# Groups of few units alternate with full ones, z gets a third buffer, and side tiles whose inputs are missing let others pass

## The chip, the cores and the metric

The kernel runs on all 8 cores of one Trainium2 chip. Each core computes half of the tokens of one of the four sequences (2048 rows out of 4096: every second block of 128), and no core talks to another. The metric is the device time of the slowest core in microseconds (us). A core has TensorE (PE in the profile), VectorE (DVE), ScalarE (ACT), GpSimd (POOL) and SyncE (SP). They run side by side and wait for each other by semaphores.

## What is computed

```python
h = rms_norm(x, g_pre)
proj = h @ w_in                                  # w_in: 1024 x 6144
q, k, v, z_a, cb, cc, cx, z_c, ga, gc = jnp.split(proj, idx, axis=-1)
# branch A: differential attention, 4 heads, two softmax maps each, ALiBi, causal
s = einsum(q, k) * scale - slope[h] * (qpos - kpos)
a = softmax(s[map 0]) - lam * softmax(s[map 1])
o = rms_norm(a @ v, subln_gain) * (1 - lam_init)
y_attn = (o * silu(z_a)) @ w_attn_o
# branch B: width-3 causal depthwise convolution, gated
u = causal_depthwise_conv(cc * cx, conv_w)
y_conv = ((cb * u) * silu(z_c)) @ w_conv_o
# merge and output
y = sigmoid(ga + b_a) * y_attn + sigmoid(gc + b_c) * y_conv
out = x + rms_norm(y @ w_out, g_post)
```

## The kernel before

The program is recorded first and played later. `Prog.op` appends an operation to the list of its engine, works out its semaphore waits from the names that it reads and writes, and keeps a rough clock of its own for each engine (`p.now`), from an assumed duration `t` for every operation. The planner's decisions (what stands next on PE, when a piece of DVE work is put in) are taken from that clock while the program is built. On the chip the order of each engine is fixed.

**Stages.** (1) Up to about 156 us: norms of x, transposes, and the projections to V, K and Q. (2) From 156 to 547 us: attention, the subject here. (3) Merge gates and branch outputs (L1428, L1435), up to 713 us. (4) Output projection (L1481) and the final norm.

**The attention stage.** Its work is cut into 16 groups, one for a stripe s of 512 query rows and a head h. A group is a run of units. One unit is a score matmul over key blocks (L1099), an exponential on ACT (L1128), on the causal edge a mask on DVE (L1140), and the product with V (L1159). Stripe 0 has 3 units; stripe 3 has 15 for heads 2 and 3. Heads 0 and 1 have steep ALiBi slopes, so their far blocks are left out and their groups are short: 3 units for (0, 0), 5 for (3, 0). `GROUPS` is the order of the groups. Scores fill PSUM banks 0 to 3, and the sums over V sit in banks 4 to 6.

**Side tiles.** ACT has more to do for a unit than PE, so PE takes other matmuls between units: tiles from one list, `fill.q`, all of which use the only bank left, bank 7. They are `kq` (L725, remaining Q and K projections), `norm` (L907, only before the fork), `conv` (L823, 8 matmuls of 512 columns, 64 tiles), `halo` (L954, 16 matmuls of 32 columns), `z` (L858, 32 matmuls of 128 columns, the silu gate's input for one group) and `trans` (L1239, 4 transposes of a group's gated output; its result is copied out at L1246). `put_fill` takes from the head of the list until PE's planned time reaches the next unit, and `credit` spreads the tiles over the stage.

**The end of a group.** `epilogue` (L1186 to L1204) sums and scales the accumulators on DVE, and must be through before the next group's L1159 may write banks 4 to 6. It then puts the rest on the list `side`: four squares (L1213), `rstd` (two small operations on DVE, L1219 and L1221, and a power on POOL, L1223), four gates (L1231), which read `oraw`, the POOL result and `sz`, and `trans`. `z` has its own tail: a tanh on ACT (L870), a multiplication (L872), later the gain (L878). Pieces of `side` and `chain` are put on DVE where the planner sees room.

**Two buffers.** `oraw`, `gat` and `sz` have two buffers, taken in turn by the number g of the group. So a group's `trans` must be done before the epilogue of the group two later, and `epilogue` begins with this:

```python
while g >= 2 and g - 2 not in t_done:
    fill.step()
```

It takes side tiles one after the other, with whatever waits they have, until `trans` of g - 2 is through. And z's tile of group g is held back in `z_wait` until nothing of group g - 2 is left on `side`, since both use the same half of `sz`:

```python
if z_wait and not any(x[0] <= g - 2 for x in side):
    fill.push(z_tile(*z_wait))
```

Up to the first four groups (heads 2 and 3, stripes 3 and 0) the norms of Q and K are measured beside the attention; behind them a register decides between two versions of the rest (the fork; its value is read behind L943). The version that runs here leaves out the far blocks.

Of the kernel before, what the change touches and what calls it, by code (L numbers as in the profile page):

```python
# [289 lines left out]
def build_program():  # L290
# [23 lines left out]
    with contextlib.ExitStack() as st:  # L314
        K = 1024
# [3 lines left out]
        def emission(p, skip):  # L319
# [14 lines left out]
            def take(n):  # L334
                nonlocal o
                r = o
                o += (n + 63) // 64 * 64
                return r
# [70 lines left out]
            sz_off = take(4 * K)  # L409
            sz = [reg(sz_off + i * 2 * K, 2 * K, F32).rearrange("p (b n) -> p b n", b=4) for i in range(2)]  # L410
            gc_off = take(16 * K)
# [10 lines left out]
            zr_off = [take(2 * K) for _ in range(2)]  # L422
            tz_off = take(2 * K)
            tz = reg(tz_off, 2 * K, F32)
            zr = [reg(a, 2 * K, F32) for a in zr_off]
# [52 lines left out]
            for i in range(2):  # L478
                for d in range(4):
                    p.place(("hTp", i, d), htp_off[i], 8 * K)  # L480
                p.apart([("hTp", i, d) for d in range(4)])
                p.place(("prod", i), pr_off[i], 2080)
                p.place(("ut", i), u_off[i], 2 * K)
                p.place(("tt", i), t_off[i], 2 * K)
                p.place(("zr", i), zr_off[i], 2 * K)
                p.place(("sz", i), sz_off + i * 2 * K, 2 * K)
            p.place(("wz",), wz_off, 8 * K)
            for i in range(2):
                for t in range(4):
                    p.place(("sq", i, t), gc_off + 8 * K + i * 4 * K + t * K, K)  # L490
            p.place(("tz",), tz_off, 2 * K)
            for i in range(NR):
                p.place(("ring", i), ring_off[i], 2 * K)
# [356 lines left out]
            def z_tile(s, h, g):  # L850
                tb = g % 2

# [38 lines left out]
            def squares_of(until):  # L891

                while pieces and not kq_left and pieces[0][0] < 2 + len(normed) and p.now["pool"] < until:
                    i, t = pieces.pop(0)
                    what, h, kd = NORMS[i]
                    src = KT[h][:, kd * 2048 + t * 512:kd * 2048 + (t + 1) * 512] if what == "k" else QT[h][:, t * 512:(t + 1) * 512]
                    name = ("KT", h, kd, t) if what == "k" else ("QT", h, t)
                    p.op("pool", (lambda e, i=i, t=t, src=src: e.tensor_tensor(out=sq[i % 2][:, t * 512:(t + 1) * 512], in0=src, in1=src, op=ALU.mult)),
                         reads=[name], writes=[("sq", i % 2, t)], t=1.35)
                    if t == 3:  # L900
                        fill.q.insert(min(1, len(fill.q)), norm_tile(i))

            def norm_tile(i):
# [9 lines left out]
                def post(bk):  # L913
                    p.op("dve", (lambda e: e.tensor_reduce(out=S_NM[:, i:i + 1], in_=bank(bk)[:, 0:32], axis=mybir.AxisListType.X, op=ALU.max)),
                         reads=[("bank", bk)], writes=[("nm", i)], t=0.2)
                    normed.append(i)
                    if i == len(NORMS) - 1:
                        for a, lo, hi in ((0, 0, 4), (1, 4, 6)):
# [118 lines left out]

            GROUPS = [(s, h) for one, two in ((3, 0), (2, 1)) for h in HEADS for s in (one, two)]

# [136 lines left out]
            def epilogue(s, h, g):  # L1176
# [49 lines left out]
                def gate(qb):  # L1226
                    while g not in z_done:
                        fill.step()
                    run_hot()
                    flush_chain(("z", g))  # L1230
                    p.op("dve", (lambda e: e.scalar_tensor_tensor(out=gat[ob][:, qb, :], in0=oraw[ob][:, qb, :], scalar=RS[:, qb:qb + 1],  # L1231
                                                                  in1=sz[ob][:, qb, :], op0=ALU.mult, op1=ALU.mult)),
                         reads=[("oraw", ob, qb), ("rs", ob), ("sz", ob)], writes=[("gat", ob, qb)], t=0.345)

                def trans():
# [8 lines left out]
                    def post(bk):  # L1244
                        t_done.add(g)
                        p.op("dve", (lambda e: e.tensor_copy(out=gattnT[:, h, s * 512:(s + 1) * 512], in_=bank_bf16(bk)[:, 0:512])),  # L1246
                             reads=[("bank", bk)], writes=[("gattnT", h, s)], t=0.43)
                    tile_ = {"mm": mm, "post": post, "n": 4, "w": 0.057}
                    if over[0]:
# [6 lines left out]
                for qb in range(4):  # L1256
                    side.append((g, 0.35, lambda qb=qb: gate(qb), [("rs", ob), ("sz", ob), ("z", g)]))
                side.append((g, 0.0, trans, []))
# [31 lines left out]
            def put_exp(n):  # L1290
                emit_exp(n)
                exp_end[n] = p.ops["act"][-1].end
                if any(x[2] for x in units[n][2]):
                    exp_end[n, "mask"] = p.ops["dve"][-1].end

            def put_fill(until):

# [5 lines left out]
                while now["pe"] < until or credit - took[0] > 0.0:  # L1303
# [5 lines left out]
                    if fill.left() <= TAIL:  # L1309
                        break  # L1310
                    one()

# [26 lines left out]

            fill.q.insert(len(kq), z_tile(*GROUPS[0], 0))  # L1340
            z_wait = None
            put_qk(0)
            put_exp(0)
            for n in range(NU):
                s, h, segs, first, last = units[n]
                if first:
                    started = set()
                    if g:
                        z_wait = (s, h, g)
                    late -= 0.057 * 4 * KC + 0.057 * 4  # L1350
                if last:
                    drain(g - 2)
                if z_wait and not any(x[0] <= g - 2 for x in side):
                    fill.push(z_tile(*z_wait))
                    z_wait = None
                credit += max(0.0, fill.left() + late - TAIL - credit) * work[n] / rest_work
# [258 lines left out]
```

How the kernel before makes its waits and increments, by code:

```python
    def replay(self, eng_name, engine, part, waited):  # L181
        cut = self.parting[eng_name]
        for o in self.ops[eng_name][:cut] if part == 0 else self.ops[eng_name][cut:]:
            need = {}
            for d in o.waits:
                s, v = d.token
                if v > need.get(s, 0):
                    need[s] = v
            for s in sorted(need):
                v = need[s]
                if waited.get(s, 0) >= v:
                    continue
                engine.wait_ge(self.sems[s], v)
                waited[s] = v
            ins = o.fn(engine)
            if o.token is not None:
                ins.then_inc(self.sems[o.token[0]], 16 if o.dma is not None else 1)
# [9 lines left out]
    def play(name, e):  # L207
        waited = {}
        r = e.alloc_register("way_" + name)
        fast.regs[name] = r
        fast.replay(name, e, 0, waited)
        with e.If_cmp(r, 1, "IS_GE"):
            fast.replay(name, e, 1, dict(waited))
        with e.If_lt(r, 1):
            general.replay(name, e, 1, dict(waited))
        if name == "sp":
            assert [o.token for o in fast.final_ops] == [o.token for o in general.final_ops]
            for o in fast.final_ops:
                e.wait_ge(fast.sems[o.token[0]], o.token[1])
```

## Time and profile before

| | us |
|---|---|
| median of 3 runs (778.79 to 782.70) | 780.42 |
| the profiled execution, its device time | 780.28 |
| its slowest core (core 4), first to last instruction | 778.7 |
| the eight cores, first to last instruction | 772.3 to 778.7 |

The profiled execution lies 0.14 us from the median, so a sum made on it stands for the median. PE is busy for 93% of the span, and no other engine for as much as half of it: PE's work, its waits and its clock make the time. The attention stage is 391 us of that span, and nearly all of PE's waits behind the start of the kernel lie in it. Times in the rows further down are core 4's.

### The profile page before, as it was taken

The page shows a single profiled execution, that of the slowest core. Times are in us where ns is not written, and L with a number is a line of the kernel's source. Part 1 is how long each engine was busy: PE and PEld are TensorE (multiplying, and loading weights), DVE is VectorE, ACT ScalarE, POOL GpSimd, SP SyncE. Part 2 cuts the span into 40 slices and gives each one's busy share as a digit, 9 for nine tenths or more (in the row PEclk, how much of TensorE's full clock was granted, in tenths as well). Part 3 has the DMA queues.
Part 4 walks back from the last instruction along what each step waited for, and adds up shares of the span by engine and source line. Part 5 has one row for each costly group of instructions (what it writes and reads, how often), then busy time and mean ns, then how long its engine had stood idle before and what let it go on. Part 6 is the DMA issues. An engine that isn't in the chain of part 4 may idle for free.

```text
span 778.7 us, 15293 instructions; the slowest of 8 cores (772.3 to 778.7 us)
## 1 busy us (share of the span) xinstructions
PE 724.1 (93%) x5370; PEld 382.2 (49%) x5370; DVE 368.8 (47%) x829; ACT 377.5 (48%) x552; POOL 152.5 (20%) x165
## 2 busy tenths in 40 slices
PE   4799999998888998799999999899999999999995
PEld 1354444455555454455555556555444444444442
DVE  3666444222654456657565467746522222222444
ACT  2446555264565654376666667675222222223433
POOL 1100000105711000010100001101333332321663
PEclk9999999998999999899999999999999999999998
DMA  7997973810000110000100101002852222200786
GB/s 166 246 209 203 252 168 68 128 22 2 2 2 29 28 18 12 2 15 15 29 2 2 28 2 28 3 1 56 134 123 41 41 42 40 42 1 1 247 293 221
DMA packets 39684, 57.68 MB, mean 74 GB/s; under 512 B 23825, under 2 KB 24209, under 8 KB 39346
## 3 DMA queue, kind: packets, MB, share of 16 engines
q1 hardware_dynamic: 31682, 39.58, 18.4%
q0 software_dynamic: 7776, 16.78, 13.8%
q8 instruction: 47, 0.77, 0.4%
q14 instruction: 35, 0.29, 0.1%
q10 hardware_dynamic: 144, 0.26, 0.1%
HBM read 59.76 MB, written 8.39 MB: 88 GB/s over the span
## 4 chain that ended last, share of the span: by engine, by line
PE 84%; DVE 7%; issue 4%; ACT 2%; DMA 1%; DVEq 0%; POOL 0%; SPq 0%; ACTq 0%; POOLq 0%
PE psum L1428 14%; PE psum L823 13%; PE psum L1159 12%; PE psum L725 11%; PE psum L711 8%; PE psum L1481 7%; PE psum L1435 7%; PE psum L1099 6%; PE psum L858 4%; ACT arena L1128 2%; DVE arena L1199 1%; PE psum L688 1%; DVE arena L1204 1%; PE psum L1239 1%; DMA arena<-gpre 1%
## 5 line engine op out<-in xcount | busy, mean ns | idle before, releaser
L1128 ACT ACTIVATE arena<-psum 128x1024 bf16<-128x1024 f32 (+2 forms) x259 | 219.0, 902 | 112.5 <-PE psum L1099 111.9
L1159 PE MATMUL psum<-arena 128*128 128x130 bf16 x1780 | 134.0, 223 | 5.3 <-DVE arena L1199 2.8
L1159 PEld LDWEIGHTS psum<-arena 128*128 128x128 bf16 x1780 | 106.0, 99 | 54.2 <-issue 47.9
L823 PE MATMUL psum<-arena 128*128 128x512 bf16 x512 | 126.3, 389 | 5.7 <-DVE arena L1186 2.1
L1428 PE MATMUL psum<-arena 128*128 128x512 bf16 x512 | 115.7, 379 | 0.0
L1440 ACT ACTIVATE arena<-psum,arena 128x512 f32<-128x512 f32 x64 | 44.0, 687 | 120.4 <-PE psum L1428 120.4
L1444 DVE SCALAR_TENSOR_TENSOR arena<-arena,psum 128x512 f32<-128x512 f32 x64 | 43.8, 687 | 115.8 <-PE psum L1435 115.8
L725 PE MATMUL psum<-arena 128*128 128x512 bf16 x384 | 88.4, 379 | 0.0
L1099 PE MATMUL psum<-arena 64*128 64x512 bf16 (+3 forms) x568 | 73.8, 340 | 6.3 <-ACT arena L1128 3.9
L1428 PEld LDWEIGHTS psum<-arena 128*128 128x128 bf16 x512 | 50.1, 98 | 60.2
L823 PEld LDWEIGHTS psum<-arena 128*128 128x128 bf16 x512 | 47.6, 99 | 54.9 <-issue 12.6
L711 PE MATMUL psum<-arena 128*128 128x512 bf16 x256 | 64.0, 394 | 5.2 <-DVE arena L643 4.2
L1447 POOL TENSOR_TENSOR arena<-arena 128x512 bf16<-128x512 f32 x32 | 40.4, 1262 | 116.6 <-DVE arena L1444 116.6
L1435 PE MATMUL psum<-arena 128*128 128x512 bf16 x256 | 60.5, 379 | 0.0
L725 PEld LDWEIGHTS psum<-arena 128*128 128x128 bf16 x384 | 37.0, 98 | 42.9 <-issue 0.4
L1481 PE MATMUL psum<-arena 128*128 128x512 bf16 x256 | 57.0, 387 | 0.0
L740 ACT CAST arena<-psum 128x512 bf16<-128x512 f32 x42 | 24.5, 584 | 58.5 <-PE psum L725 58.5
L1223 POOL TENSOR_TENSOR arena<-arena 128x4 f32<-128x4 f32 x16 | 18.8, 1176 | 148.1 <-DVE arena L1221 142.8
L716 DVE TENSOR_TENSOR arena<-psum,arena 128x512 bf16<-128x512 f32 x32 | 22.1, 691 | 51.6 <-PE psum L711 51.4
L645 DVE SCALAR_TENSOR_TENSOR arena<-arena 128x1024 bf16<-128x1024 f32 (+1 forms) x33 | 42.4, 1284 | 3.4
L711 PEld LDWEIGHTS psum<-arena 128*128 128x128 bf16 x256 | 25.0, 100 | 37.0 <-issue 9.8
L630 ACT ACTIVATE arena<-arena 128x1024 bf16<-128x1024 f32 (+1 forms) x33 | 34.9, 1058 | 15.1 <-DMA arena<-x_perm 15.1
(101 smaller groups left out, 626.3 us busy)
## 6 DMA issues: line engine op xcount, KB each, us to landing
arena<-x_perm SPq DMA_DIRECT2D x48, 512.0 KB, 6.4
arena<-w_chunk POOLq DMA_DIRECT2D x40, 256.0 KB, 4.8
out_own<-arena SPq DMA_DIRECT2D x15, 512.0 KB, 4.7
arena<-w_y POOLq DMA_DIRECT2D x8, 256.0 KB, 5.5
arena<-wo_r POOLq DMA_DIRECT2D x1, 2048.0 KB, 20.6
arena<-w_wide POOLq DMA_DIRECT2D x4, 256.0 KB, 11.4
arena<-w_wide POOLq DMA_DIRECT2D x1, 1024.0 KB, 11.9
arena<-gpost SPq DMA_DIRECT2D x1, 512.0 KB, 3.6
```

The source lines that it names most:

```text
L645: p.op("dve", (lambda e: e.scalar_tensor_tensor(out=xn[nb][0:rows, :], in0=xring[b][0:rows, :], scalar=rs0[0:rows, n:n + 1], in1=gpre[0:ro ...
L711: p.op("pe", (lambda e, kc=kc: e.matmul(bank(bk), lhsT=h_blk(n, kc), rhs=wv[kc // 2][:, kc % 2, :], start=(kc == 0), stop=(kc == KC - 1))) ...
L725: p.op("pe", (lambda e: e.matmul(bank(bk), lhsT=w[:, kc, :], rhs=rhs, start=(kc == 0), stop=(kc == KC - 1))), reads=[("w" + what, h)] + h_ ...
L823: p.op("pe", (lambda e: e.matmul(bank(bk), lhsT=lhs(kc), rhs=rhs(kc), start=(kc == 0), stop=(kc == n - 1))), reads=rd, writes=[("bank", bk)])
L1099: p.op("pe", (lambda e, kd=kd, m=m, kcol=kcol, q0=q0, c0=c0, w=w: e.matmul(psum[:, 2 * kd + m, c0 * 128:(c0 + w) * 128], lhsT=KT[h][64 * m ...
L1128: p.op("act", (lambda e, a0=a0, a1=a1, c0=c0, c1=c1, bias=bias: e.activation(out=PT[sl][:, a0:a1, c0 * 128:c1 * 128], in_=psum[:, a0:a1, c ...
L1159: p.op("pe", (lambda e, kd=kd, m=m, cb=cb, acc=acc, first=first, vj=vj: e.matmul(acc, lhsT=PT[sl][:, 2 * kd + m, cb * 128:(cb + 1) * 128], ...
L1428: p.op("pe", (lambda e, sl=sl, bk=bk, kc=kc: e.matmul(bank(bk), lhsT=ring[sl][:, kc, :], rhs=hTo[:, kc, t * 512:(t + 1) * 512], start=(kc ...
L1435: p.op("pe", (lambda e, br=br, bk=bk, c=c, src=src: e.matmul(bank(bk), lhsT=ring[sy][:, 4 * br + c, :], rhs=src[:, c, t * 512:(t + 1) * 51 ...
L1440: p.op("act", (lambda e, br=br: e.activation(out=tmp[ts[br]], in_=bank(bs[br]), func=AF.Tanh, scale=0.5, bias=bm[:, 8 * br + j:8 * br + j ...
L1444: p.op("dve", (lambda e, br=br: e.scalar_tensor_tensor(out=tmp[ts[br]], in0=tmp[ts[br]], scalar=1.0, in1=bank(bs[2 + br]), op0=ALU.add, op ...
L1481: p.op("pe", (lambda e, j=j, half=half: e.matmul(bank(b0 + half), lhsT=yT[:, j, i * 128:(i + 1) * 128], rhs=wo[:, j, half * 512:(half + 1) ...
```

## The change

1. The order of the groups from the fifth on: a group of few units no longer follows another one where a longer one can stand between.
2. `sz` gets a third buffer (`NZ = 3`, 2 KB in each partition, at the end of the side region), and z's tile goes to the head of the list at the first unit of its group; `z_wait` is gone.
3. `trans` says what it needs (`need`: the four gated blocks). `next_ready`, called before a side tile is begun in `put_fill`, looks at the tile at the head: if its inputs come more than 0.1 us later than PE's planned time, the first tile without `need` is put in front of it.
4. The pieces of the norm measurement no longer count on being finished in order (`normed` is looked up by number).

The matmuls, the vector operations, the transfers and their sizes are the same ones; only order and the place of one buffer change.

```diff
-            GROUPS = [(s, h) for one, two in ((3, 0), (2, 1)) for h in HEADS for s in (one, two)]
+            GROUPS = [(3, 2), (0, 2), (3, 3), (0, 3)]
+
+            GROUPS += [(3, 0), (2, 2), (0, 0), (3, 1), (0, 1), (2, 3), (2, 0), (1, 2), (1, 0), (2, 1), (1, 3), (1, 1)]
...
+            NZ = 3
+            sz_at = [sz_off, sz_off + 2 * K, take(2 * K)]
...
-                tb = g % 2
+                tb = g % NZ
...
-                    tile_ = {"mm": mm, "post": post, "n": 4, "w": 0.057}
+                    tile_ = {"mm": mm, "post": post, "n": 4, "w": 0.057, "need": [("gat", ob, qb) for qb in range(4)]}
...
+            def next_ready():
+
+                if p.when(fill.q[0].get("need", [])) > now["pe"] + 0.1:
+                    later = [k for k, t in enumerate(fill.q) if "need" not in t]
+                    if later:
+                        fill.q.insert(0, fill.q.pop(later[0]))
...
                     if fill.left() <= TAIL:
                         break
+                    if not fill.open:
+                        next_ready()
                     one()
...
                     if g:
-                        z_wait = (s, h, g)
+                        fill.push(z_tile(s, h, g))
...
-                if z_wait and not any(x[0] <= g - 2 for x in side):
-                    fill.push(z_tile(*z_wait))
-                    z_wait = None
```

The order before was (3,2) (0,2) (3,3) (0,3) | (3,0) (0,0) (3,1) (0,1) (2,2) (1,2) (2,3) (1,3) (2,0) (1,0) (2,1) (1,1), as (stripe, head), with the fork at the bar.

Code lines behind the additions have other numbers after: L823 is L826, L858 is L861, L984 is L987, L1099 is L1104, L1159 is L1164, L1213 is L1218, L1221 is L1226, L1231 is L1236, L1239 is L1244, L1246 is L1251.

**The first place: PE at the end of group (3, 0),** number 4. Before, the end of a `conv` tile, the last masked product of its unit but one, scores, the group's last products, and what `epilogue` makes PE take:

```order
L823 MATMUL psum<-arena 128x512 x8
L1159 MATMUL psum<-arena 128x130 x4
L1099 MATMUL psum<-arena 128x512 x4
L1159 MATMUL psum<-arena 128x130 x8
L858 MATMUL psum<-arena 128x128 x32
L1239 MATMUL psum<-arena 128x128 x4
L823 MATMUL psum<-arena 128x512 x8
```

and after:

```order
L826 MATMUL psum<-arena 128x512 x4
L1164 MATMUL psum<-arena 128x130 x4
L1104 MATMUL psum<-arena 128x512 x4
L1164 MATMUL psum<-arena 128x130 x8
L826 MATMUL psum<-arena 128x512 x4
L1244 MATMUL psum<-arena 128x128 x4
L826 MATMUL psum<-arena 128x512 x8
```

The z tile (32 matmuls) has left the place ahead of `trans` of group 2; half of a `conv` tile stands there now. `trans` is still taken by `epilogue`.

**The second place: PE around `trans` of group 3, (0, 3).** Before, at the end of the three-unit group (0, 0), with the first scores of the group that follows:

```order
L1159 MATMUL psum<-arena 128x130 x8
L858 MATMUL psum<-arena 128x128 x32
L1239 MATMUL psum<-arena 128x128 x4
L823 MATMUL psum<-arena 128x512 x8
L1099 MATMUL psum<-arena 128x256 x4
```

After, inside the 11-unit group (2, 2):

```order
L826 MATMUL psum<-arena 128x512 x8
L1104 MATMUL psum<-arena 128x256 x4
L1164 MATMUL psum<-arena 128x130 x16
L1244 MATMUL psum<-arena 128x128 x4
L1104 MATMUL psum<-arena 128x512 x4
L1164 MATMUL psum<-arena 128x130 x4
L826 MATMUL psum<-arena 128x512 x8
```

`trans` has moved from right behind z's tile to between two units, and no `conv` tile follows it directly.

**The third place: DVE at the first place.** Before:

```order
L1140 TENSOR_TENSOR arena<-arena 128x4x128
L1213 SCALAR_TENSOR_TENSOR arena<-arena 128x128
L984 TENSOR_TENSOR arena<-psum,arena 128x4x128
L1213 SCALAR_TENSOR_TENSOR arena<-arena 128x128 x2
L1219 SCALAR_TENSOR_TENSOR arena<-arena 128x4
L1221 TENSOR_TENSOR arena<-arena 128x4
L1231 SCALAR_TENSOR_TENSOR arena<-arena 128x128 x4
L872 SCALAR_TENSOR_TENSOR arena<-arena,psum 128x512
L1246 COPY arena<-psum 128x512
```

After:

```order
L1145 TENSOR_TENSOR arena<-arena 128x4x128
L1218 SCALAR_TENSOR_TENSOR arena<-arena 128x128 x2
L1224 SCALAR_TENSOR_TENSOR arena<-arena 128x4
L1226 TENSOR_TENSOR arena<-arena 128x4
L881 TENSOR_TENSOR arena<-arena 128x512
L1236 SCALAR_TENSOR_TENSOR arena<-arena 128x128 x4
L987 TENSOR_TENSOR arena<-psum,arena 128x4x128
L1251 COPY arena<-psum 128x512
```

The squares no longer stand around a `conv` tile's L984 (now L987), which has moved behind the gates, and z's L872 has left the row between gates and copy.

## Rows read from the trace of the kernel before

**Rows 1.** The page: busy us of each engine, share of the span, instructions.
```profile
PE 724.1 (93%) x5370; PEld 382.2 (49%) x5370; DVE 368.8 (47%) x829; ACT 377.5 (48%) x552; POOL 152.5 (20%) x165
```

**Rows 2.** Stretches of core 4: length, busy us by engine, PEclk, DMA share, GB/s.
```profile
156.00:282.00 126.00, 114.26 (x1152) 69.72 (x1151) 55.06 (x129) 73.56 (x84) 31.48 (x32) 0.93 0.06 13
282.00:324.00 42.00, 33.72 (x293) 18.53 (x292) 26.51 (x75) 16.02 (x28) 3.49 (x6) 0.88 0.09 14
324.00:404.00 80.00, 77.36 (x823) 46.98 (x820) 51.12 (x149) 54.98 (x65) 9.40 (x13) 1.00 0.09 15
404.00:547.00 143.00, 133.71 (x1384) 80.45 (x1383) 82.79 (x239) 92.42 (x117) 12.37 (x19) 1.00 0.09 16
```

**Rows 3.** PE's waits, 156 to 547 us: for whom, us in total, times, longest.
```profile
PE psum L1239 <- DVE arena L872: 7.2, 5, 3.6
PE psum L1099 <- ACT arena L1128: 3.9, 12, 1.0
```

**Rows 4.** Timeline, first place: start, us, engine, instructions [idle before <-releaser].
```profile
294.27 0.35 DVE L1213 SCALAR_TENSOR_TENSOR arena<-arena 128x128 f32<-128x128 f32 x1
294.40 1.89 PE L823 MATMUL psum<-arena 128*128 128x512 bf16 x8
...
297.00 0.34 DVE L1213 SCALAR_TENSOR_TENSOR arena<-arena 128x128 f32<-128x128 f32 x1
...
297.45 1.95 PE L858 MATMUL psum<-arena 128*128 128x128 bf16 x32
...
299.71 1.14 DVE L1231 SCALAR_TENSOR_TENSOR arena<-arena 128x128 bf16<-128x128 f32 x4 [1.35 <-POOL arena L1223]
...
301.03 0.69 DVE L872 SCALAR_TENSOR_TENSOR arena<-arena,psum 128x512 f32<-128x512 f32 x1 [0.18 <-DVE arena L1231]
...
301.87 0.38 PE L1239 MATMUL psum<-arena 128*128 128x128 bf16 x4 [2.47 <-DVE arena L872]
...
302.93 3.19 PE L823 MATMUL psum<-arena 128*128 128x512 bf16 x8 [0.68 <-DVE arena L1186]
```

**Rows 5.** Timeline, second place, the same columns.
```profile
312.70 1.95 PE L858 MATMUL psum<-arena 128*128 128x128 bf16 x32
...
316.07 1.14 DVE L1231 SCALAR_TENSOR_TENSOR arena<-arena 128x128 bf16<-128x128 f32 x4 [1.31 <-POOL arena L1223]
...
318.22 0.58 PE L1239 MATMUL psum<-arena 128*128 128x128 bf16 x4 [3.57 <-DVE arena L872]
...
319.48 3.57 PE L823 MATMUL psum<-arena 128*128 128x512 bf16 x8 [0.68 <-DVE arena L1186]
```

**Rows 6.** Timeline of PE: other `trans` tiles, and the `conv` tile behind one.
```profile
386.41 1.00 PE L1239 MATMUL psum<-arena 128*128 128x128 bf16 x4 [0.64 <-DVE arena L1231]
...
405.35 0.39 PE L1239 MATMUL psum<-arena 128*128 128x128 bf16 x4
406.42 0.59 PE L823 MATMUL psum<-arena 128*128 128x512 bf16 x2 [0.68 <-DVE arena L1246]
...
420.88 1.00 PE L1239 MATMUL psum<-arena 128*128 128x128 bf16 x4 [0.52 <-DVE arena L1231]
```

**Rows 7.** Timeline of PE: a group's start behind `halo`, and one behind no tile.
```profile
271.47 0.39 PE L1159 MATMUL psum<-arena 128*128 128x130 bf16 x4 [0.48 <-DVE arena L1199]
...
272.92 3.42 PE L858 MATMUL psum<-arena 128*128 128x128 bf16 x32
...
493.05 0.50 PE L1159 MATMUL psum<-arena 128*128 128x130 bf16 x6 [0.58 <-DVE arena L1199]
494.10 0.50 PE L1159 MATMUL psum<-arena 128*128 128x130 bf16 x6 [0.56 <-DVE arena L1204]
```

**Rows 8.** A wait of PE on its timeline, and two stretches of 10 us as in Rows 2.
```profile
235.16 1.04 PE L1099 MATMUL psum<-arena 64*128 64x512 bf16 x4 [1.84 <-DVE arena L943]
...
230.00:240.00 10.00, 7.92 (x80) 5.51 (x78) 4.54 (x16) 4.33 (x5) 1.40 (x1) 0.83 0.13 53
480.00:490.00 10.00, 8.45 (x115) 6.10 (x115) 8.79 (x30) 6.83 (x12) 1.01 (x1) 1.00 0.01 2
```

More of the change, by code:

```diff
@@ L409, in emission @@
             sz_off = take(4 * K)
-            sz = [reg(sz_off + i * 2 * K, 2 * K, F32).rearrange("p (b n) -> p b n", b=4) for i in range(2)]
             gc_off = take(16 * K)
@@ L423, in emission @@
             tz_off = take(2 * K)
+            NZ = 3
+            sz_at = [sz_off, sz_off + 2 * K, take(2 * K)]
+            sz = [reg(a, 2 * K, F32).rearrange("p (b n) -> p b n", b=4) for a in sz_at]
             tz = reg(tz_off, 2 * K, F32)
@@ L485, in emission @@
                 p.place(("zr", i), zr_off[i], 2 * K)
-                p.place(("sz", i), sz_off + i * 2 * K, 2 * K)
             p.place(("wz",), wz_off, 8 * K)
@@ L491, in emission @@
             p.place(("tz",), tz_off, 2 * K)
+            for i in range(NZ):
+                p.place(("sz", i), sz_at[i], 2 * K)
             for i in range(NR):
@@ L891, in squares_of @@
             def squares_of(until):
-                while pieces and not kq_left and pieces[0][0] < 2 + len(normed) and p.now["pool"] < until:
+                while pieces and not kq_left and (pieces[0][0] < 2 or pieces[0][0] - 2 in normed) and p.now["pool"] < until:
                     i, t = pieces.pop(0)
@@ L916, in post @@
                     normed.append(i)
-                    if i == len(NORMS) - 1:
+                    if len(normed) == len(NORMS):
                         for a, lo, hi in ((0, 0, 4), (1, 4, 6)):
@@ L1231, in gate @@
                     p.op("dve", (lambda e: e.scalar_tensor_tensor(out=gat[ob][:, qb, :], in0=oraw[ob][:, qb, :], scalar=RS[:, qb:qb + 1],
-                                                                  in1=sz[ob][:, qb, :], op0=ALU.mult, op1=ALU.mult)),
-                         reads=[("oraw", ob, qb), ("rs", ob), ("sz", ob)], writes=[("gat", ob, qb)], t=0.345)
+                                                                  in1=sz[g % NZ][:, qb, :], op0=ALU.mult, op1=ALU.mult)),
+                         reads=[("oraw", ob, qb), ("rs", ob), ("sz", g % NZ)], writes=[("gat", ob, qb)], t=0.345)
                 def trans():
@@ L1256, in epilogue @@
                 for qb in range(4):
-                    side.append((g, 0.35, lambda qb=qb: gate(qb), [("rs", ob), ("sz", ob), ("z", g)]))
+                    side.append((g, 0.35, lambda qb=qb: gate(qb), [("rs", ob), ("sz", g % NZ), ("z", g)]))
                 side.append((g, 0.0, trans, []))
@@ L1352, in emission @@
                     drain(g - 2)
-                if z_wait and not any(x[0] <= g - 2 for x in side):
-                    fill.push(z_tile(*z_wait))
-                    z_wait = None
                 credit += max(0.0, fill.left() + late - TAIL - credit) * work[n] / rest_work
```

## The prediction

> **What bounds the kernel now.** Start with the page's busy times: PE has 724.1 us of a 778.7 us span, DVE, ACT and POOL under half each [rows 1]. So a change of order can only win what PE waits, or what it runs at its lower clock. The table of stretches says where that is [rows 2]. From 156 to 547 us PE is busy for 359 of 391 us, so 32 us are idle. They are not spread evenly: 282 to 324 us holds 8.3 us of idle time in 42 and a granted clock of 0.88, while the next 80 us hold 2.6 us and run at the full 2.4 GHz. The table of waits names the largest one: `trans` (L1239) behind z's L872, 7.2 us in five waits, the longest 3.6 [rows 3]. The timeline shows two of the five carrying 6.0 us: 2.47 at 301.9 and 3.57 at 318.2 [rows 4, 5].
>
> The reader should see the same chain in both. `epilogue` may not start before `trans` of group g - 2 is through, so PE takes z's tile and `trans` at once. DVE is still at that old group: squares, POOL's power, four gates, and only then z's L872, which frees bank 7. `trans` needs the gates and the bank, so it waits for all of it. The `conv` tile behind it waits 0.68 for the copy of `trans` out of bank 7. After so much idle time PE is granted 1.2 GHz: 8 matmuls take 3.19 and 3.57 us [rows 4, 5], where they take 1.89 at 2.4 GHz [rows 4].
>
> **The sum,** against the profiled execution's 780.28 us (0.14 under the median). The work on every engine is the same; all terms are waits, the clock, and the pace of PE.
>
> A, the first place, `trans` of (3, 3) at the end of (3, 0). It stays forced. Without z's tile PE gets to it when it got to z's, 297.45 [rows 4], since the `conv` half moved in behind the scores is the half taken out ahead of them. On DVE the two squares now follow the mask at once, without L984 between them. Two squares to the end of the gates took 297.00 to 300.85, 3.85 us [rows 4]. From 294.27 that makes 298.1. L987 follows with 0.18 + 0.69 (the step and duration of L872 [rows 4]), and 0.15 to release: 299.1. The wait is 1.65 instead of 2.47: **-0.8**. The 0.68 behind it stays. Whether the low clock goes is open: a wait of 1.84 alone, at 235.16, stands in a stretch at 0.83, and 1.55 us of idle time in shorter waits, 480 to 490 us, in one at 1.00 [rows 8]. 1.65 plus 0.68 is nearer to the first, so I keep the low clock. Bounds: 0, and -2.1 with it gone (another 3.19 - 1.89 = 1.3).
>
> B, the second place, `trans` of (0, 3). After, the eleven units of (2, 2) give DVE time: `trans` stands between two units with three `conv` tiles ahead of it since the end of (3, 0), and scores follow it, not a `conv` tile. I count the wait as gone (3.57), the wait for the copy (0.68), and the low clock: 0.58 - 0.38 on `trans`, 3.57 - 1.89 on the tile behind [rows 4, 5]. **-6.1**. Bounds: -6.1, and -4.3 if a low clock comes elsewhere instead.
>
> C, `trans` tiles begun before their gates are done. Three (one more between the two shown) waited 0.64, 0.52 and 0.21, and then ran at the pace of the gates, 1.00 us each where a ready one takes 0.38 [rows 6]. `next_ready` puts a `conv` or `halo` tile in front while the gates run. 1.37 + 3 x 0.62 = **-3.2**. What is late next is the DVE operation that those gates delayed, which nobody on PE awaits at once. Bounds: -3.2, and -1.4 if only the waits go.
>
> D, bank 7. A `conv` tile directly behind `trans` waits 0.68 [rows 6]. The order has five such pairs before (two are in A and B) and six after (one in A): three against five outside. 2 x 0.68 = **+1.4**. Bounds: +0.7 to +2.
>
> E, the starts of groups. The first products wait for `epilogue`: a full `conv` tile between hides that, `halo` leaves 0.7 or so, nothing between leaves 0.58 + 0.56 [rows 7]. Before, `halo` stands at two such ends and no tile at one. After, `halo` stands at one, no tile at two ((2, 0) and (1, 0)), and only the short `trans` at (1, 3). One `halo` less, two bare starts more, at 1.14 each less what a shorter wait takes off: between 0 and +2.3, I take **+1.0**, since at (2, 0) more PE work stands ahead of the next group's first products than at the bare start shown. The `halo` that goes is the one before the z tile of 3.42 us [rows 7], which ran at 1.2 GHz; 1.95 is the warm value [rows 4]. That would be another -1.5. Since two new places of idle time could bring a fall of the clock, I count neither.
>
> F, PE waiting for ACT at scores: 3.9 us in twelve waits [rows 3]. Short groups come more often between long ones, and where DVE and PE no longer stall, ACT's exponentials come next. Bounds 0 and +1: **+0.5**.
>
> The third z buffer costs nothing by itself: its 2 KB lie behind everything else in the side region, and what is loaded over that region later does not reach it. z's tile at the first unit takes 1.8 us of PE in any case. Its cover is the `conv` tiles that move behind it; were they not there, each early z tile would bring its L872 into the way of the next tile in bank 7.
>
> -0.8 - 6.1 - 3.2 + 1.4 + 1.0 + 0.5 = -7.2, so **773.1 us**.
>
> **The rivals.** 1. *The clock recovers more than I count.* The low clock at A goes and the one at 272.9 as well: -7.2 - 1.3 - 1.5, 770.3 us, and down to 769 with E at zero. For it: both follow waits that shrink. Against: 235.16, where one wait of 1.84 was enough. 0.13.
>
> 2. *The waits only move.* One bank for all side tiles is the real limit. C comes back as waits for bank 7 (its 3.2 not won), D and E stand at their upper ends (+0.6, +1.3): -2.1, 778.2 us. For it: each reordered tile still needs the last tile's eviction, and DVE is busy for 26.5 of 42 us around the two places [rows 2]. Against: between 324 and 404 us with the same bank PE idles only 2.6 us [rows 2]. 0.14. The Trainium skill speaks for this rival: its page Perfetto Trace Analysis, section Matmuls, wants independent matmul groups to rotate through different PSUM banks so that eviction overlaps the next group, and this change adds an SBUF buffer and no bank. The 0.68 behind `trans` agrees with that page.
>
> 3. *Short waits keep the clock down.* B's 1.9 comes back at another place, and one bare start brings a fall as at 230 to 240 (0.17 of 10 us, 1.7): -7.2 + 1.9 + 1.7, 776.7 us. For it: the z tile of 3.42 us followed nothing longer than 0.48 [rows 7]. Against: 324 to 547 us has waits of all these kinds at 1.00 [rows 2]. 0.07. The Trainium skill describes this in TensorE: Matmul & The Clock Gate, section A second HAM failure mode: many micro-idles between groups that cycle through PSUM make the clock swing. Up to 324 us the trace here agrees, behind it not.
>
> 4. *Slower: passing makes `trans` late.* A `trans` that lets tiles pass stays undone; if it is still undone at the epilogue two groups on, it is forced there, in front of a DVE queue full of the old group's work. The price is B's 6.1 each time. The places are the ends of (0, 0), (2, 0) and (1, 0), where the group before is short. Twice makes -7.2 + 12.2, 785.3 us. It decides from the point where the gates run more than about two side tiles later than planned. Against: the three waits of C say that the gates end within 0.6 us of where they were awaited. 0.04.
>
> The change could also do nothing at all where it matters, if `next_ready` never acted. The order shows `trans` at new places, so I fold that into rival 2.
>
> **How the numbers follow.** The forecast, 773.1, has 0.62. Its own bounds run from -10 to -4 by B, C, D and E, 770.3 to 776.3. The range takes in rivals 1 and 3 and the near side of rival 2: 769 to 778. 0.5% of 780 us is 3.9 us, about what a measurement tells from no change. Faster by more is below 776.5: 0.62 + 0.13 + half of rival 3, **0.79**. Within 0.5%: rival 2 and the other half, **0.17**. Slower: **0.04**.
>
> **What would show it.** A: at the end of (3, 0), L1244 with a wait near 1.65, and 8 matmuls behind it at 3.2 or 1.9 us. B: no wait over 0.3 before L1244 inside (2, 2), and the granted clock of the stretch at 0.93 or more. C: no L1244 waiting for L1236, each x4 at 0.38. D: five waits of 0.68 at L826 behind L1244 outside A. E: waits at L1164 behind L1204 or L1209 at the ends of (2, 0), (1, 0) and (1, 3). The whole stage should be 383 to 384 us long instead of 391. The prediction is wrong if PE's idle time between 156 and its end stays near 32 us, or if L1244 has any wait over 2 us other than A's.

## The result, and the profile after

The changed kernel takes 769.58 us (median of four runs, 769.11 to 770.96) against 780.42: a ratio of 0.9886, 95% interval 0.9862 to 0.9910. The forecast was 773.1, the range 769 to 778. The profiled execution took 770.96 us, and its slowest core is core 1. Executions in which the cores of one die show a lower granted clock than the others (809.36 us, once, of the kernel before) are left out of every time here.

The lines of the attention stage have numbers 3 to 5 higher now. `trans` is L1244 (was L1239), the gates L1236 (L1231), z's matmuls L861 and its multiplication L875, `conv` L826, the copy of `trans` out of bank 7 L1251, scores L1104, the product with V L1164, the exponential L1133.

The page of the changed kernel: busy us, share of the span, instructions; below them the granted clock in 40 slices. The rows answer to [rows 1].

```profile
PE 715.8 (93%) x5370; PEld 378.7 (49%) x5370; DVE 368.6 (48%) x829; ACT 377.7 (49%) x552; POOL 152.6 (20%) x165
...
PEclk9999999998998999999999999999999999999998
```

PE's busy time fell by 8.3 us although it executes the same matmuls: the same work ran at a higher clock, or no longer at the pace of what it waits for. The stretches of core 1 (columns as in [rows 2]) say where:

```profile
156.00:282.00 126.00, 114.61 (x1155) 68.41 (x1153) 56.22 (x128) 70.99 (x81) 31.00 (x33) 0.93 0.08 15
282.00:324.00 42.00, 37.85 (x380) 22.54 (x376) 28.48 (x85) 26.30 (x35) 5.06 (x7) 1.00 0.09 14
324.00:404.00 80.00, 75.04 (x809) 46.20 (x809) 49.36 (x140) 54.15 (x67) 7.78 (x11) 1.00 0.10 15
```

The stretch from 282 to 324 us, which had 8.3 us of idle time and a clock of 0.88, has 4.1 us and 1.00. The quiet stretch behind it got a little worse: 5.0 us idle in 80 where it had 2.6. From 156 us to the end of attention (540 us here) PE is idle for 29.5 us, where it had 32.0.

How long is the attention stage on each core, from its first score matmul to the first matmul of the merge stage? Before, 386.2 to 390.5 us, median 388.6. After, 378.7 to 382.2, median 380.2. The merge stage behind it takes 166.0 us in both, and what follows that, 64.7 and 64.6 us. So all 8.4 us come from the stage that the change touches.

The two places of the argument. PE's timeline of core 1 (columns as in [rows 4]):

```profile
277.96 1.95 PE L861 MATMUL psum<-arena 128*128 128x128 bf16 x32 [0.21 <-DVE arena L987]
...
301.09 0.38 PE L1244 MATMUL psum<-arena 128*128 128x128 bf16 x4 [1.41 <-DVE arena L987]
...
302.15 1.89 PE L826 MATMUL psum<-arena 128*128 128x512 bf16 x8 [0.68 <-DVE arena L1191]
...
317.69 0.39 PE L1244 MATMUL psum<-arena 128*128 128x128 bf16 x4
318.01 0.61 PE L1104 MATMUL psum<-arena 64*128 64x512 bf16 x4
```

The first place has a shorter wait, 1.41 for 2.47 [rows 4]. The second `trans`, at 317.69, has none where it had 3.57 [rows 5], and scores stand behind it instead of a `conv` tile that needs bank 7. The z tile at 277.96 takes 1.95 us; its counterpart took 3.42 [rows 7], nearly all of it at 1.2 GHz (granted clock 0.54 from 272.9 to 276.3 us).

PE's waits on core 1, 156 to 540 us (for whom, us in total, times, longest), against [rows 3]:

```profile
PE psum L1104 <- ACT arena L1133: 5.1, 13, 0.8
...
PE psum L826 <- DVE arena L1251: 3.4, 5, 0.7
...
PE psum L1164 <- DVE arena L1204: 3.1, 6, 1.1
...
PE psum L826 <- DVE arena L875: 1.8, 6, 0.6
...
PE psum L1244 <- DVE arena L987: 1.4, 1, 1.4
...
PE psum L1244 <- DVE arena L1019: 0.8, 2, 0.4
...
PE psum L1244 <- DVE arena L875: 0.6, 1, 0.6
```

The row that led the table before, `trans` behind z's multiplication with 7.2 us, is down to 0.6. No `trans` waits for the gates (L1236) any more. What leads now is scores waiting for ACT, 5.1 us against 3.9.

### The profile page after: what moved, and what is told of

It is laid out like the page before. It is cut to its first block, busy times and chain, and to the rows that moved or that the text cites. A ratio compares the mean times of both kernels' runs of the same rounds, so it can differ in the third digit from the quotient of the medians.

```text
span 769.4 us, 15277 instructions; the slowest of 8 cores (765.9 to 769.4 us)
## 1 busy us (share of the span) xinstructions
PE 715.8 (93%) x5370; PEld 378.7 (49%) x5370; DVE 368.6 (48%) x829; ACT 377.7 (49%) x552; POOL 152.6 (20%) x165
## 4 chain that ended last, share of the span: by engine, by line
PE 82%; DVE 7%; issue 4%; DMA 3%; ACT 2%; POOL 0%; DVEq 0%; ACTq 0%; SPq 0%; POOLq 0%
PE psum L1438 14%; PE psum L826 13%; PE psum L1164 12%; PE psum L728 10%; PE psum L1491 7%; PE psum L1445 7%; PE psum L714 7%; PE psum L1104 6%; PE psum L861 4%; DMA arena<-w_wide 2%; ACT arena L1133 1%; DVE arena L1204 1%; DMA arena<-arena 1%; DVE arena L875 1%; DVE arena L1209 1%
## 5 line engine op out<-in xcount | busy, mean ns | idle before, releaser
L1133 ACT ACTIVATE arena<-psum 128x1024 bf16<-128x1024 f32 (+3 forms) x259 | 219.0, 902 | 112.5 <-PE psum L1104 108.9
L1164 PE MATMUL psum<-arena 128*128 128x130 bf16 x1780 | 134.3, 223 | 5.8 <-DVE arena L1204 3.1
L1164 PEld LDWEIGHTS psum<-arena 128*128 128x128 bf16 x1780 | 105.9, 99 | 55.5 <-issue 48.5
L826 PE MATMUL psum<-arena 128*128 128x512 bf16 x512 | 123.9, 384 | 7.2 <-DVE arena L1251 3.4
L1104 PE MATMUL psum<-arena 64*128 64x512 bf16 (+3 forms) x568 | 73.2, 338 | 7.4 <-ACT arena L1133 5.1
L826 PEld LDWEIGHTS psum<-arena 128*128 128x128 bf16 x512 | 47.2, 99 | 56.0 <-issue 12.9
```

The source lines that it names most:

```text
L826: p.op("pe", (lambda e: e.matmul(bank(bk), lhsT=lhs(kc), rhs=rhs(kc), start=(kc == 0), stop=(kc == n - 1))), reads=rd, writes=[("bank", bk)])
L1104: p.op("pe", (lambda e, kd=kd, m=m, kcol=kcol, q0=q0, c0=c0, w=w: e.matmul(psum[:, 2 * kd + m, c0 * 128:(c0 + w) * 128], lhsT=KT[h][64 * m ...
L1133: p.op("act", (lambda e, a0=a0, a1=a1, c0=c0, c1=c1, bias=bias: e.activation(out=PT[sl][:, a0:a1, c0 * 128:c1 * 128], in_=psum[:, a0:a1, c ...
L1164: p.op("pe", (lambda e, kd=kd, m=m, cb=cb, acc=acc, first=first, vj=vj: e.matmul(acc, lhsT=PT[sl][:, 2 * kd + m, cb * 128:(cb + 1) * 128], ...
```

## The experiments

The change has three parts that can be built apart: **order** (the new `GROUPS`), **passing** (`next_ready`) and **early z** (the third buffer of `sz`, with z's tile pushed at the group's first unit). Six kernels, with before and after, make all eight combinations. Each was compared with the kernel before on the same chip. "Stage" is the attention stage of the profiled execution, median of its eight cores; "cores" is the span of all cores, averaged over the executions. The kernel before has two values there: 775.8 beside e1, e2, e3 and e5, 774.2 beside e4 and e6, which were timed later. A stage is read from one execution: for e3, e4 and e5 it is the quickest that was taken, for e6 and the changed kernel the slowest, so differences between stages are good to about 1 or 2 us.

| kernel | order | passing | early z | ratio (95%) | stage, us | cores, us |
|---|---|---|---|---|---|---|
| before | | | | 1 | 388.6 | 775.8, 774.2 |
| e1_z_alone | | | x | 1.0034 (1.0021 to 1.0048) | 390.4 | 778.4 |
| e2_pass_alone | | x | | 1.0012 (0.9996 to 1.0028) | 387.9 | 776.4 |
| e3_order_alone | x | | | 0.9966 (0.9948 to 0.9983) | 382.2 | 771.0 |
| e4_no_third_z | x | x | | 0.9957 (0.9938 to 0.9977) | 383.8 | 771.1 |
| e5_no_pass | x | | x | 1.0029 (1.0011 to 1.0048) | 389.2 | 778.6 |
| e6_old_order | | x | x | 0.9958 (0.9939 to 0.9976) | 385.9 | 772.5 |
| after | x | x | x | 0.9886 (0.9862 to 0.9910) | 380.2 | 766.6 |

**Early z alone (e1_z_alone):** `GROUPS` as before, and the call of `next_ready` taken out.

```diff
-                    if not fill.open:
-                        next_ready()
```

> The kernel before with the third z buffer and the early z tile alone: old order of groups, no passing. My theory (each part has its own stall; a z tile at the first unit is only a move): both forced trans tiles stay, since the short groups (0, 0) and (0, 3) still leave DVE no time, so the waits of 2.5 and 3.6 us and the low clock behind them remain; within 1 us of before. Rival 1 (the third buffer is what frees the order): at least 3 us faster. Rival 2 (an early z tile puts its own DVE work in front of gates, so more trans tiles wait): 2 to 4 us slower, with more than three waits at trans behind the gates.

Measured: slower, by 2.7 us, as rival 2 had it: four `trans` tiles wait for the gates, and seven of the fifteen in the stage run at 0.8 us or more. PE's timeline of core 7 at the two places (`trans` is L1242 here, the gates L1234):

```profile
298.48 1.00 PE L1242 MATMUL psum<-arena 128*128 128x128 bf16 x4 [1.89 <-DVE arena L1234]
...
300.16 3.28 PE L826 MATMUL psum<-arena 128*128 128x512 bf16 x8 [0.68 <-DVE arena L1189]
...
312.92 1.05 PE L1242 MATMUL psum<-arena 128*128 128x128 bf16 x4 [3.56 <-DVE arena L1234]
```

With z's tile out of the way, PE reaches `trans` earlier and waits for the gates themselves. The four transposes then run at the gates' pace, 1.00 us for 0.38. The wait has a new name and the old size. In the old order z's tile was not the cause of these two waits; the queue of the old group's work on DVE was.

**Passing alone (e2_pass_alone):** `GROUPS`, the two buffers and `z_wait` as before; `next_ready` and `need` stay.

> The kernel before with the passing alone: old order of groups, two z buffers. My theory: term C and nothing else, 3.2 us off before (no trans at the pace of the gates, each four at 0.38 us), while both forced waits stay, because epilogue takes trans without asking. Rival (passing matters little, since a trans that is passed is forced later): within 1 us of before, with a third forced wait over 1 us.

Measured: 1.0012, no difference that can be told. The time is the rival's, but no third forced wait appeared. Two rows of core 1's timeline around a `trans` that had waited 0.21 and run for 1.00 us in the kernel before (core 0, the slowest, lacks 78 matmul records, and a lost record lengthens the wait shown before the next one):

```profile
346.96 0.39 PE L1242 MATMUL psum<-arena 128*128 128x128 bf16 x4
...
348.03 0.59 PE L826 MATMUL psum<-arena 128*128 128x512 bf16 x2 [0.68 <-DVE arena L1249]
```

and its table of waits:

```profile
PE psum L1242 <- DVE arena L875: 7.2, 5, 3.6
PE psum L1102 <- ACT arena L1131: 4.9, 13, 1.1
PE psum L826 <- DVE arena L1249: 3.7, 5, 1.0
...
PE psum L826 <- DVE arena L1189: 2.1, 3, 0.7
```

`next_ready` does what it says: no `trans` runs at the gates' pace any more. That takes 3.1 us off the waits and the pace of `trans`. But the `conv` tiles directly behind `trans` now wait for bank 7 for 5.1 us in all, where they waited 3.4 before, and scores wait 4.9 us for ACT instead of 3.9. Together with smaller waits that gives back the 3.1. The two forced waits (2.47 and 3.57 us) cannot be passed, since `epilogue` pulls `trans` in front of everything.

**Order alone (e3_order_alone):** two z buffers, `z_wait` as before, no call of `next_ready`.

> The kernel before with the new order of groups alone: two z buffers with the old hold, no passing. My theory: term B, 6.1 us off before, less 0.5 to 1 for the starts of groups, so 5 to 6 us off; the wait of 3.6 us gone, the first forced one of about 2.5 us still there with the low clock behind it, and the trans tiles at the pace of the gates remain. Rival (order works only together with the third buffer, since a long group between short ones holds the z tile back): under 2 us off, a forced wait of over 2 us at a new place.

Measured: 0.9966, 2.6 us at the slowest core (3.8 between the medians), although the stage is 6.4 us shorter and the mean core 4.8 us faster. The theory's 5 to 6 us did not come at the slowest core, and the rival's new forced wait did not appear. The profiled execution is the quickest of the eight. On core 3 the second forced wait is gone and the first stands as it was:

```profile
302.88 0.38 PE L1244 MATMUL psum<-arena 128*128 128x128 bf16 x4 [2.47 <-DVE arena L875]
...
303.94 1.89 PE L826 MATMUL psum<-arena 128*128 128x512 bf16 x8 [0.68 <-DVE arena L1191]
```

So the order by itself removes the 3.57. The executions spread from 773.9 to 778.6 us; the last section comes back to that.

**All but the third buffer (e4_no_third_z):**

```diff
-            NZ = 3
-            sz_at = [sz_off, sz_off + 2 * K, take(2 * K)]
+            NZ = 2
+            sz_at = [sz_off, sz_off + 2 * K]
```

and `z_wait` back as before.

> The changed kernel with two z buffers and the old hold on z's tile; new order and passing stay. The runs so far: order alone -0.3%, third buffer with order but no passing +0.3%, all three -1.1%. Theory (order carries the gain, and passing is needed only to bear the early z tiles): near the order alone, 775 to 778 us, with the wait of 2.5 us at the first place back, since z's tile stands ahead of the forced trans again. Rival (passing is what the order lacked, and the third buffer is a minor part): 769 to 772 us.

Measured: 0.9957, 5.5 us behind the changed kernel by the ratios, and 775.6 us, as the theory had it. Core 2's wait at the first place is the old one again, and scores wait 6.6 us for ACT in all:

```profile
299.69 0.56 PE L1244 MATMUL psum<-arena 128*128 128x128 bf16 x4 [2.47 <-DVE arena L875]
...
300.92 2.98 PE L826 MATMUL psum<-arena 128*128 128x512 bf16 x8 [0.68 <-DVE arena L1191]
```

**All but passing (e5_no_pass):** only the call of `next_ready` taken out.

> The changed kernel without the passing: new order and third z buffer. My theory: term C comes back, 3.2 us slower than the changed kernel, still 5 to 7 us faster than before. Rival (early z tiles make passing necessary, since more trans tiles stand at the head of the list before their gates are done): 5 to 8 us slower than the changed kernel, with five or more waits at trans behind the gates.

Measured: 1.0029, slower than before, and 11 us slower than the changed kernel by the ratios: more than even the rival expected. PE's waits for the gates and two `trans` tiles on core 6:

```profile
PE psum L1244 <- DVE arena L1236: 4.1, 4, 1.9
```

```profile
408.20 1.00 PE L1244 MATMUL psum<-arena 128*128 128x128 bf16 x4 [0.93 <-DVE arena L1236]
...
476.83 1.00 PE L1244 MATMUL psum<-arena 128*128 128x128 bf16 x4 [0.87 <-DVE arena L1236]
```

Eleven of the sixteen `trans` tiles run at 0.8 us or more; that pace costs 6.7 us beside the 4.1 of waits. With early z and short groups, `trans` stands at the head of the list while its gates run, at nearly every group. This is the experiment that shows the parts are not a sum: passing is worth 0.7 us of stage alone and 9.0 us on top of the other two. The mean core says the same: 0.6 us slower alone, 12.0 us faster on top.

**All but the order (e6_old_order):** `GROUPS` as before.

> The changed kernel in the old order of groups; third buffer and passing stay. Theory: both forced trans tiles are back, since (0, 0) and (0, 3) leave DVE no time; they cost about what the first place costs now plus the second place's 6.1 us: 776 to 780 us, with waits over 1.4 and 3 us at trans. Rival (an early z tile is enough to disarm the forced trans of the second place too): 772 us or less.

Measured: 0.9958, 776.5 us, inside the theory's range. On core 5 both places are still there, shorter (waits of 1.41 and 2.63 us), `conv` tiles directly behind `trans` wait 5.4 us in all (4.1 in the changed kernel) and scores behind ACT 7.1 (5.1).

**Only (2, 2) moved (e7_only_22):** the changed kernel, with (2, 2) between (3, 0) and (0, 0) and all other groups as before.

```diff
-            GROUPS += [(3, 0), (2, 2), (0, 0), (3, 1), (0, 1), (2, 3), (2, 0), (1, 2), (1, 0), (2, 1), (1, 3), (1, 1)]
+            GROUPS += [(3, 0), (2, 2), (0, 0), (3, 1), (0, 1), (1, 2), (2, 3), (1, 3), (2, 0), (1, 0), (2, 1), (1, 1)]
```

> The changed kernel with only one move in the order: (2, 2) stands between (3, 0) and (0, 0), the rest as before. Theory (the second place is what the order is worth): within 2 us of the changed kernel, 769 to 772 us, no trans with a wait over 2 us. Rival (the alternation further on carries as much): 774 us or more.

Measured: 0.9881 (0.9838 to 0.9923), 770.0 us, the changed kernel's time, as the theory had it. Core 2's waits:

```profile
PE psum L1104 <- ACT arena L1133: 7.5, 16, 1.4
...
PE psum L1244 <- DVE arena L987: 1.4, 1, 1.4
```

With the other two parts in place, one long group in one place carries the whole worth of the new order. Alternating the later groups as well gives nothing that this comparison can tell: waits for ACT are 7.5 us here and 5.1 in the changed kernel, but products with V wait 2.8 here and 4.8 there, and `conv` directly behind `trans` 3.4 and 4.1.

**Another order (e8_searched_order).** What remains of the first place is a short group, (3, 0), directly behind the short (0, 3). This order puts two long groups there:

```diff
-            GROUPS += [(3, 0), (2, 2), (0, 0), (3, 1), (0, 1), (2, 3), (2, 0), (1, 2), (1, 0), (2, 1), (1, 3), (1, 1)]
+            GROUPS += [(2, 3), (2, 2), (1, 0), (1, 2), (0, 0), (3, 0), (3, 1), (2, 1), (1, 3), (2, 0), (0, 1), (1, 1)]
```

> The changed kernel in another order behind the fork: (2,3) (2,2) (1,0) (1,2) (0,0) (3,0) (3,1) (2,1) (1,3) (2,0) (0,1) (1,1). A long group stands directly behind the four first ones, so no trans is forced at the first place: its wait of 1.4, the 0.7 behind it and the low clock that half of the cores showed there go, and fewer trans tiles are followed by a conv tile. Theory: 4 to 6 us faster than the changed kernel, 764 to 766 us. Rival (the forced trans only moves to a later short group, (0, 1) or (2, 0)): within 2 us of the changed kernel, with a wait over 1 us at a trans there.

Measured: 765.49 us (764.56 to 765.70), 0.982 (0.9778 to 0.9862), stage 373.9, mean core 761.0: faster than both kernels, and inside the theory's 764 to 766. Core 7's waits, and the stretch that was the worst:

```profile
PE psum L826 <- DVE arena L1251: 3.4, 5, 0.7
...
PE psum L1104 <- ACT arena L1133: 2.5, 9, 0.5
...
PE psum L1244 <- DVE arena L875: 0.2, 1, 0.2
```

```profile
282.00:324.00 42.00, 39.34 (x388) 22.97 (x386) 25.56 (x73) 26.78 (x32) 3.80 (x6) 1.00 0.08 14
```

No `trans` is forced while its inputs are missing; all its waits together are 0.31 us. Idle time in the stretch is 2.7 us of 42.

**That order with two z buffers (e9_searched_two_z), and without passing (e10_searched_no_pass).** Are the other two parts still needed where no `trans` is forced? e9 is e8 with the diff of e4, e10 is e8 with the diff of e1.

> The searched order of the run before (765.5 us) with two z buffers and the old hold on z's tile; passing stays. Theory (the third buffer pays where a z tile would otherwise stand ahead of a forced trans, and this order forces none early): it costs less than the 6 us that it cost in the changed kernel's order, 766 to 769 us. Rival (the third buffer is worth its 6 us in any order): 771 us or more.

> The searched order with the third z buffer but without the passing. Theory (early z tiles make DVE late, so every trans that may not let others pass waits for its gates, in any order): 8 to 14 us slower than with passing, 774 to 780 us, most trans tiles at 1.00 us instead of 0.38. Rival (passing is needed only where short groups stand close together): under 4 us slower.

Both of my theories fell. I had expected the third buffer to be worth at most 4 us there. Measured: 0.9976 (0.9953 to 0.9998), 777.9 us, 12 us slower than e8, 7 of them in the attention stage (380.7 for 373.9). PE on core 3:

```profile
408.62 1.95 PE L861 MATMUL psum<-arena 128*128 128x128 bf16 x32 [0.94 <-DVE arena L1009]
412.34 0.38 PE L1244 MATMUL psum<-arena 128*128 128x128 bf16 x4 [1.77 <-DVE arena L875]
...
515.23 0.38 PE L1244 MATMUL psum<-arena 128*128 128x128 bf16 x4 [1.71 <-ACT arena L1133]
...
548.01 0.38 PE L1244 MATMUL psum<-arena 128*128 128x128 bf16 x4 [1.94 <-DVE arena L1019]
...
548.61 5.30 PE L1442 MATMUL psum<-arena 128*128 128x512 bf16 x16 [0.21 <-DVE arena L1009]
```

and DVE on the same core, the last gate and z's multiplication:

```profile
405.68 0.34 DVE L1236 SCALAR_TENSOR_TENSOR arena<-arena 128x128 bf16<-128x128 f32 x1
...
411.50 0.69 DVE L875 SCALAR_TENSOR_TENSOR arena<-arena,psum 128x512 f32<-128x512 f32 x1 [3.03 <-ACT arena L873]
```

Held-back z tiles bring forced waits back at new places, two in the stage. Here z's tile is the cause: the gates had ended 6.3 us before the first of these `trans` tiles and 4.5 us before the second, and both waited for L875, which waited for z's tanh on ACT. (The second wait carries the name of an exponential, but L875 ended last, at 515.09.) A third wait, 1.94 us, falls in the merge stage between two `trans` tiles and has a low clock behind it (5.30 us for 3.62), which makes that stage 170.4 us instead of 166.0.

And I had expected passing to be needed in that order as much as in the changed kernel. Without it the ratio is 0.9874 (0.9789 to 0.9958), from three executions with a median of 772.0 us; by the ratios that is 4 us slower than e8, between the theory's 8 to 14 and the rival's "under 4", with an interval that holds nearly all of them. The stage is 377.1, 3.2 us longer than e8's; the same step cost 9.0 us in the changed kernel. So the order decides how much each part is worth: in e8's the third buffer carries more and, by the stage, passing less.

## Why the prediction was right, and where it was not

Sorted by who waits for whom, PE's rows on the slowest core of each profile give the terms as they came out. Waits before and after, in us:

| | before | after |
|---|---|---|
| `trans` before it starts | 8.56 | 2.85 |
| `trans` at the gates' pace, over 0.38 each | 2.18 | 0.32 |
| `conv` directly behind `trans` | 3.40 | 4.08 |
| scores behind ACT | 3.95 | 5.14 |
| products with V | 4.45 | 4.80 |
| other `conv` | 2.08 | 2.86 |
| z | 0.21 | 0.97 |
| all of PE's waits and the gates' pace, other rows included | 31.7 | 28.1 |
| full `conv` and z tiles, us over their time at full clock | 7.47 | 3.26 |

**A, right, a little better.** Forced as before, 1.41 instead of the 1.65 predicted. From the first square (296.25) to the start of `trans` (301.09) pass 4.84 us, where the forecast had 4.83; PE got there a quarter of a microsecond later than counted. DVE on core 1:

```profile
296.25 0.34 DVE L1218 SCALAR_TENSOR_TENSOR arena<-arena 128x128 f32<-128x128 f32 x1
...
299.21 1.14 DVE L1236 SCALAR_TENSOR_TENSOR arena<-arena 128x128 bf16<-128x128 f32 x4 [1.00 <-POOL arena L1228]
300.26 0.68 DVE L987 TENSOR_TENSOR arena<-psum,arena 128x512 f32<-128x512 f32 x1
```

**B, right in full.** In the changed kernel: no wait, no `conv` behind it, clock 1.00 in the stretch (at least 0.93 was asked for). e3 shows that the order alone does it, and e7 that moving (2, 2) alone does it where the other two parts stand.

**C, right as an observation, wrong as a term of its own.** No `trans` waits for the gates, and nearly all run in 0.38, as forecast. But I booked 3.2 us for it as if it were independent of everything else. In e2 the same mechanism acts and brings nothing: of the 3.1 us that PE no longer loses at `trans`, 1.7 come back as waits for bank 7 behind it and 1.0 as waits of scores for ACT. And in the changed kernel passing is worth 9.0 us, since early z puts `trans` next to its gates far more often. The failed step is the sentence that nobody on PE awaits the DVE operation that the gates delay. Rival 2 had that mechanism; the rows of products with V, other `conv` and z, +0.35, +0.78 and +0.76, and the 5.0 us of idle time between 324 and 404 us, where 2.6 stood, are its share here. (The third of the `trans` tiles that C counts stands at 345.86 us, ahead of the two shown, not between them; the sum is not touched.) The page Perfetto Trace Analysis of the Trainium skill, section Matmuls, asks for independent groups in rotating PSUM banks. e2 agrees with it, with 5.1 us of waits behind `trans` for the only bank; no run here has a second bank for side tiles.

**D, right.** Six waits of 0.68 behind `trans`, five outside A (240.58, 261.96, 366.40, 410.70, 528.15 us). 4.08 less 3.40 is the +0.68 that remains of +1.4 when B's pair is counted here.

**E, too dear, and from a row misread.** 0.4 us instead of 1.0. PE's timeline at two starts, behind (1, 0) and later, behind (1, 3), after a `trans`:

```profile
461.35 1.24 PE L826 MATMUL psum<-arena 128*128 128x512 bf16 x5
...
463.50 0.50 PE L1164 MATMUL psum<-arena 128*128 128x130 bf16 x6 [0.58 <-DVE arena L1204]
464.56 0.50 PE L1164 MATMUL psum<-arena 128*128 128x130 bf16 x6 [0.56 <-DVE arena L1209]
...
516.17 1.56 PE L1164 MATMUL psum<-arena 128*128 128x130 bf16 x16 [0.65 <-DVE arena L1204]
```

The first has the full 1.14 us, but neither it nor the start of before that has the same waits [rows 7] is bare: five of the eight matmuls of a `conv` tile, 1.24 us, stand between the old group's last products and the new group's first scores in both (at 490.90 us before). It is the same start, behind (1, 0), so it adds nothing to the difference. The others behind the fork stayed below 0.75. At (2, 0) the same five matmuls stand in between, and the wait is 0.18, since longer scores follow them (0.79 us for 0.39).

**F, right in sign, too small.** 1.2 us instead of 0.5.

**The clock, mis-sized.** Waits and pace together gave -3.6 us, where my terms without clock come to -5.35 (-0.8 - 4.25 - 3.2 + 1.4 + 1.0 + 0.5). The last row of the table gives -4.2, where I had counted -1.9 in B. The surplus of 2.3 is for the most part the z tile at 272.9, whose 1.5 us I named and left out for fear of new falls at bare starts, and the tile at A, 1.3 us, warm on this core but not on four of the eight. No new falls came: on core 1 the clock is 1.00 from 282 us on. So a gain too large on the side of the waits and one too small on the side of the clock nearly cancel, and the sum comes to -7.8 for the -7.2 forecast. This is rival 1 in part. Rival 3 fell. How near the two errors came to each other is luck. The cores' mean clock was 0.977 to 0.985 before and is 0.985 to 0.991. The same split shows in the idle time, which I had named as a sign: it fell from 32.0 to 29.5 us. That is nearer to the 32 of the sign than to a gain of 7, and within 1 us of the 28.5 that the terms for waits alone come to (-0.8 - 4.25 - 1.4 + 1.4 + 1.0 + 0.5).

**What is left over.** The stages of the two cores differ by 9.1 us. The 1.3 us beyond -7.8 lie in rows too short for this sorting, and stay open. The profiled executions differ by 9.3, and the median of the changed kernel lies another 1.4 below its profiled execution: together the 3.5 us by which the forecast was too high, within its range. The bounds of -10 to -4 in "How the numbers follow" are not the sum of the bounds of B, C, D and E: added up with A and F as forecast, these give -8.9 to -1.7. The range rested on the rivals, and the result lies within 1 us of its lower end.

**Rival 4** did not happen, in the changed kernel or in e2, where passing stands alone. e9 has forced waits at new places, but in the stage they come from z's tile ahead of `trans`, with the gates long done, and not from the queue of gates that this rival described.

Of the third buffer I had said that it costs nothing by itself, its cover being the `conv` tiles that move behind z's. e1 has those tiles too and shows +1.8 us of stage, 2.7 at the slowest core: the cover that it needs is passing.

## What to carry to other kernels

When the order of one queue is the cause of a wait, moving the thing that waits may only rename it, as e1 shows; put long work between the producer and the forced point instead, and look for the one place that pays, as (2, 2) did. Parts that free a resource earlier can be losses alone and gains together, so price them in combination: the same buffer moved the stage by +1.8 us alone, by -3.6 on top of the others, and by -6.8 in another order. And read the clock of the tiles behind a wait with the wait: about half of this gain, 4.2 of 7.8 us on the cores compared, was tiles that ran at full speed again.

## What the runs showed of the hardware

**The same wait brings the low clock on one core and not on the next.** The changed kernel in one execution, PE at the first place, core 0 and then core 2:

```profile
297.84 0.38 PE L1244 MATMUL psum<-arena 128*128 128x128 bf16 x4 [1.42 <-DVE arena L987]
298.90 1.89 PE L826 MATMUL psum<-arena 128*128 128x512 bf16 x8 [0.68 <-DVE arena L1191]
```

```profile
298.67 0.38 PE L1244 MATMUL psum<-arena 128*128 128x128 bf16 x4 [1.42 <-DVE arena L987]
299.73 3.39 PE L826 MATMUL psum<-arena 128*128 128x512 bf16 x8 [0.68 <-DVE arena L1191]
```

The waits are equal to 0.01 us, and the eight matmuls behind them differ by 1.50 us. Counted over all cores of nine profiles, a wait before `trans` followed by 0.68 brought the low clock on 24 of 24 cores at 3.56 to 3.58 us, on 8 of 8 at 2.63, on 24 of 32 at 2.47, and on 13 of 24 at 1.41. At 1.89 with the transposes at the gates' pace it was 16 of 16. e9, a tenth profile, has it on 5 of 8 cores at 1.77 and on none of 8 at 1.71. At 1.41 it was 4, 1 and 7 of the 8 cores of the three kernels. So the longest waits always brought it, and below that the length alone does not decide.

**What this costs a metric that takes the slowest of eight cores is open.** If each core may lose 1.5 us with a chance of about a half, and independently of the others, one of eight nearly always does, and the metric pays nearly in full. That would fit e3: the mean core is 4.8 us faster, the slowest 2.6 to 3.8, and the executions spread over 4.7 us. But the changed kernel goes the other way: its mean core is about 8 to 9 us faster and its slowest 10.8, although four of its cores still had the low clock at the first place. So it is not shown.
